# One LayerNorm's three reductions moved one output block later, and an input mean made without VectorE's help

## What is computed

```
h = layer_norm(x, ln_in_g, ln_in_b)
for each of 2 layers:
    z = h @ w_in                                  # 2048 columns, split into 8 parts
    A: a_val * sigmoid(a_gate) -> depthwise conv, width 31 -> layer_norm -> silu
    B: u = gelu(b_u); v = layer_norm(gelu(b_v), ln_v_g, ln_v_b); u * (tril(w_s) @ v + b_s)
    C: c_b * conv3(c_c * c_x)
    D: (trailing window means - token) @ w_pool * pool_scale
    h = layer_norm(ALPHA * h + concat(A, B, C, D) @ w_out)
    h = layer_norm(ALPHA * h + ffn(h))            # layer 0 dense SwiGLU, layer 1 eight experts, top 2
```

## Time and profile before

| | |
|---|---|
| time, median of 3 runs | 1467.56 us (1467.43 to 1468.27) |
| time of the profiled execution | 1467.36 us |
| its span, first to last instruction | 1465.6 us |
| TensorE matmul busy | 1451.2 us, 99% |
| weight loads into TensorE busy | 1259.8 us, 86% |
| VectorE busy | 1226.8 us, 84% |
| ScalarE busy | 962.8 us, 66% |
| GpSimd busy | 117.5 us, 8% |
| memory traffic | 300 GB/s over the span |
| mean granted TensorE clock | 0.999 of full speed |

### The profile page before, as it was taken

One profiled execution on the slowest core, in us unless ns is written; L12 is line 12 of the kernel. 1 busy time (PEld: TensorE's weight loads), 2 busy tenths in 40 slices (PEclk: granted clock), 3 DMA queues, 4 the chain that ended last, 5 costly groups with the idle time before them and its releaser, 6 DMA issues.

```text
span 1465.6 us, 20270 instructions
## 1 busy us (share of the span) xinstructions
PE 1451.2 (99%) x7821; PEld 1259.8 (86%) x7821; DVE 1226.8 (84%) x1206; ACT 962.8 (66%) x912; POOL 117.5 (8%) x131
## 2 busy tenths in 40 slices
PE   9999999999999999999999999999999999999998
PEld 8979999999997888888888888888888888788887
DVE  7987555555698899998999888898889899999886
ACT  5755333334475677777777777777777777777774
POOL 3522000000024000001000001000000101200000
PEclk9999999999999999999999999999999999999999
DMA  9736544454343699999999999999999999999991
GB/s 352 166 119 205 174 151 167 151 174 168 108 136 132 231 376 393 364 390 394 387 367 385 371 384 367 419 363 380 374 367 392 398 376 398 401 368 364 375 375 64
DMA packets 68601, 440.48 MB, mean 301 GB/s; under 512 B 9568, under 2 KB 13600, under 8 KB 17184
## 3 DMA queue, kind: packets, MB, share of 16 engines
q1 hardware_dynamic: 60464, 424.69, 76.7%
q0 software_dynamic: 5120, 13.37, 3.0%
q10 hardware_dynamic: 2928, 1.18, 0.4%
HBM read 432.12 MB, written 7.09 MB: 300 GB/s over the span
## 4 chain that ended last, share of the span: by engine, by line
PE 91%; DVE 5%; ACT 2%; issue 1%; DMA 0%; POOL 0%; DVEq 0%; SPq 0%; ACTq 0%; POOLq 0%
PE bank L951 60%; PE bank L607 22%; PE bank L755 4%; PE bank L989 2%; DVE w_lo L1427 1%; DVE w_lo L2077 1%; DVE work L1633 1%; ACT w_hi L1116 0%; PE bank L941 0%; PE bank L932 0%; DMA h<-in_x_t 0%; ACT h_tok_hi L1286 0%; DVE r_tok L2041 0%; ACT w_hi L1352 0%; PE bank L542 0%
## 5 line engine op out<-in xcount | busy, mean ns | idle before, releaser
L2077 DVE TENSOR_TENSOR w_lo<-ring,w_hi 128x2048 fp32r<-128x2048 f32 x320 | 731.2, 2290 | 79.7 <-ACT w_hi L1352 76.5
L1352 ACT ACTIVATE w_hi<-ring 128x2048 fp32r<-128x2048 f32 x320 | 613.5, 1918 | 163.4 <-PE bank L951 163.2
L951 PE MATMUL bank<-w_hi,x_hi 128*128 128x512 f32 x896 | 354.1, 395 | 1.5 <-DVE w_lo L2077 1.3
L951 PE MATMUL bank<-w_hi,x_lo 128*128 128x512 f32 x896 | 349.3, 390 | 0.0
L951 PE MATMUL bank<-w_lo,x_hi 128*128 128x512 f32 x896 | 348.5, 389 | 0.0
L951 PEld LDWEIGHTS bank<-w_hi,x_hi 128*128 128x128 f32 x896 | 168.3, 188 | 36.6 <-issue 1.9
L951 PEld LDWEIGHTS bank<-w_hi,x_lo 128*128 128x128 f32 x896 | 168.2, 188 | 35.8
L607 PE MATMUL bank<-x_hi,w_hi 128*128 128x290 f32 x656 | 196.4, 299 | 0.5 <-DVE w_lo L1427 0.5
L951 PEld LDWEIGHTS bank<-w_lo,x_hi 128*128 128x128 f32 x896 | 168.4, 188 | 33.2
L607 PE MATMUL bank<-x_lo,w_hi 128*128 128x290 f32 x656 | 195.1, 297 | 0.0
L607 PE MATMUL bank<-x_hi,w_lo 128*128 128x290 f32 x656 | 194.7, 297 | 0.0
(11 more groups left out here) (327 smaller groups left out, 1731.9 us busy)
## 6 DMA issues: line engine op xcount, KB each, us to landing
ring<-in_w_e_gate SPq DMA_DIRECT2D x112, 1024.0 KB, 7.2
ring<-in_w_e_up SPq DMA_DIRECT2D x112, 1024.0 KB, 7.3
ring<-in_w_e_down SPq DMA_DIRECT2D x112, 1024.0 KB, 7.3
ring<-in_w_in SPq DMA_DIRECT2D x15, 1024.0 KB, 5.0
ring<-in_w_ff_gate SPq DMA_DIRECT2D x14, 1024.0 KB, 4.9
ring<-in_w_ff_up SPq DMA_DIRECT2D x14, 1024.0 KB, 4.9
ring<-in_w_ff_down SPq DMA_DIRECT2D x14, 1024.0 KB, 4.9
ring<-in_w_out SPq DMA_DIRECT2D x8, 1024.0 KB, 7.7
```

Source lines behind the costliest of these rows:

```text
L951: ins = mm(out, x, w[slot][:, columns], start=(first and n == 0), stop=(last and n == 2), skip_group_check=True)
L1352: A(w_hi[(CUT0 + p) % SPLIT][:, :], ring[(START + p) % SLOTS][:, :], ACT.Copy).then_inc(hi_done, 1)
L2077: V.tensor_tensor(w_lo[(CUT0 + p) % SPLIT][:, :], ring[(START + p) % SLOTS][:, :], w_hi[(CUT0 + p) % SPLIT][:, :].bitcast(F32), ALU.subtra ...
```

## The change

The input mean takes all eight blocks by TensorE alone; VectorE's three additions and the semaphore between them are gone. In both layers the three reductions of the v norm stand behind blocks 8, 10 and 12, where they stood behind 7, 9 and 11. VectorE's list in the mixer is as it was.

```
-                for b in left if summed else range(KB // 2) if name == "in" else range(nb):
+                for b in left if summed else range(nb):
                     ready(b)
                     last = mm(bank[MEAN_BANK[name]][:, 0:TOKENS], ones[:, :], x[:, b, :],
                               start=(b == 0 and not summed), stop=(b == left[-1] if summed else b == nb - 1))
-                if name == "in":
-                    pe.wait_ge(x_summed, KB // 2 - 1)
-                    last = mm(bank[MEAN_BANK[name]][:, 0:TOKENS], ones[:, :], sq[:, 0, :], start=False, stop=True)
...
-                for n in range(4, 8):
+                for n in range(4, 14):
                     z_block(layer, n, c0)
-                next(ln_v)
-                for n in range(8, 10):
-                    z_block(layer, n, c0)
-                next(ln_v)
-                for n in range(10, 12):
-                    z_block(layer, n, c0)
-                next(ln_v)
-                for n in range(12, 14):
-                    z_block(layer, n, c0)
+                    if n in (8, 10, 12):
+                        next(ln_v)
...
-            dve.wait_ge(x_in[1], 16)
-            for b in range(KB // 2 + 1, KB):
-                if b > KB // 2 + 1:
-                    dve.wait_ge(x_summed, b - KB // 2 - 1)
-                V.tensor_tensor(sq_l[:, 0, :], h[:, KB // 2, :] if b == KB // 2 + 1 else sq_l[:, 0, :], h[:, b, :],
-                                ALU.add).then_inc(x_summed, 1)
```

More of the change, by code:

```diff
@@ L332, in build @@
         h_scaled, h_done, sq_summed = sem("h_scaled"), sem("h_done"), sem("sq_summed")
-        x_summed = sem("x_summed")
         ln_spread = sem("ln_spread")
```

## The result

The changed kernel takes 1470.55 us (median of 18 runs, 1469.82 to 1471.77), the kernel before 1467.66 us (18 runs, 1467.33 to 1468.27): ratio 1.0020, 95% interval 1.0014 to 1.0027, 2.9 us slower. The forecast was +1.8.

What follows compares the result with a forecast made beforehand. TensorE was taken to bound the kernel, with VectorE nearly full beside it in the first mixer. Input mean 0.73, layer 0 0.45 and layer 1 0.6 made +1.8 us on 1467.36: 1469.2 us, range 1466.5 to 1470.8.

Steps and rivals of the forecast that it cites:

- its own case: Whole kernel: input mean and both mixers together cost 1.8 us, giving 1469.2 us, range 1468.2 to 1470.2; chance 61%.
- the uncushioned rival: Mixers: TensorE's slack before the a means is missing, VectorE's delay goes through whole, +3.2 us, 1470.6 us; chance 9%.
- the input's share: Launch: four new matmuls replace VectorE's additions, the input mean is ready 0.73 us later and everything behind it moves.
- The contention rival: Mixers: delayed VectorE has one or two more taps per layer slowed by GpSimd, up to 0.52 us each; chance 8%.
- The stalls before the v mean: Both mixers: block 8 fills TensorE's wait for VectorE's pair sum, removing 0.91 us in layer 0 and 0.69 in layer 1.
- block 12: Both mixers: TensorE waits 0.8 us there for VectorE's late cut of the low weight part.
- the spread's move: Mixers: three transposes one block later cost nothing, since pooling covers VectorE between its cut and the scaling.
- The a norm of layer 0: Layer 0: late pair sum starts the a mean 0.35 us later, plus 0.1 after a stall: +0.45 us.
- The rival that counts the removed stalls in full: Mixers: removed stalls of 0.91 and 0.69 us count whole against the input's +0.73, giving 1466.5 us; chance 16%.
- Layer 1, the same way: Layer 1 mixer: variance 1.62 us late, a mean 0.49 later after slack, plus 0.1 for the stall: +0.6 us.
- TensorE's slack of 1.13: Layer 1: time between when VectorE's pair sum would allow the a mean and its start, absorbing part of VectorE's delay.
- the upper bound 1.26: Input mean: price of the four new matmuls if they ran like the first eight records' 2.51 us, instead of 0.73.

Runs made afterwards that it cites:

- the second experiment: The kernel before with only the v norm's reductions moved behind blocks 8, 10 and 12, input mean as before: 1469.93 us, ratio 1.0015.
- the input edit: The changed kernel with the v norm back behind blocks 7, 9 and 11, so only the input mean by TensorE alone: 1469.12 us, ratio 1.0009.
- the thinned changed kernel: The changed kernel with GpSimd's 24 side additions cut to one column each: 1468.25 us, ratio 1.0004.
- the two with one late reduction: Kernel before with only the v mean behind block 8: 1468.96 us; or with only the variance behind block 10: 1471.73 us.
- the cold kernel before: The kernel before without the eight warm-up matmuls TensorE runs before x lands: 1469.41 us, ratio 1.0011.
- the last two: Kernel before, input sum split five blocks TensorE, three VectorE, v mean mid-block 8: in layer 1 only 1466.48 us; in both layers 1467.52 us.
- the kernel with the mean in mid-block: The kernel before with the v mean in the middle of block 8 in both layers, the rest as before: 1466.88 us, ratio 0.9996.

## Why the prediction was nearly right

The forecast was 1469.2 us in a range to 1470.8, no change beyond 0.2%. The measured ratio, 1.0020, stands on that very bound, at +2.9 instead of +1.8, and the median lies within the range. It lies outside the 1468.2 to 1470.2 that the prediction gave its own case, though: the range reached so far only for the uncushioned rival (1470.6), whose sign, an a mean of layer 0 over 0.9 later than the input's share, measured 0.39. The contention rival's 1470.2 to 1471.3 holds the median, and its cause was there. So the forecast's place within the range is in part luck. Step by step:

**Right, with their sizes.** The stalls before the v mean are gone. Centring is late by 0.42 in layer 0 and 0.70 in layer 1 (forecast 0.40 and 0.61), the variance by 1.11 and 1.66 (0.88 and 1.62), TensorE stands 0.95 and 0.7 at block 12 (0.8), the spread's move costs nothing: VectorE's scaling starts at 435.02 without idle time before it. The a norm of layer 0 has moved by 0.49 (0.45). The rival that counts the removed stalls in full is out: with its cause alone the second experiment is slower by 2.3 us.

**Right in size, in part by another cause.** The variance of layer 0 is late, but the row has no wait: six taps took 1.44 longer beside GpSimd's masks. Without that VectorE would have come at 51.4 and waited for the sum, which ended at 52.54 (51.89 + 0.65). The sum by itself makes 0.8 of the 1.11, as forecast, and the slowed taps added only 0.3.

**Mis-sized: layer 1.** The step "Layer 1, the same way" had +0.6 for the a mean and the trace has +1.26. It carried the variance's delay to the a pair sum and took off TensorE's slack of 1.13, with all VectorE work between as long as before. The runs put 1.09 us more there, of VectorE beside GpSimd's additions, and a stand of 0.9 in the output projection, which TensorE doesn't get back. So the a mean of layer 1 was set by TensorE and not, as forecast, by VectorE's pair sum, which was itself 2.09 late instead of 1.62. The contention rival named this cause, by one or two taps of 0.52 in each layer. What was missing is that it is not a matter of one more tap that meets an addition: a whole stretch goes over from GpSimd slowed to VectorE slowed, and it did so in one layer of the changed kernel and not in the other.
The Trainium skill, in "SBUF — State Buffer", section "Who interferes with whom", has "Issue order, not op shape, decides who blocks". The traces agree in so far as the same instructions are slowed now on one side and now on the other, additions at 0.95 us each beside taps at 0.44, or additions at 0.79 beside taps at 0.82; that the order of issue decides it, no run here shows.

**Mis-sized: the input mean.** Forecast +0.73 at 0.247 us a record. The four new matmuls did run at 0.24 a record; the first eight did not keep their 2.51 us. The cost is 0.4 to 0.6 with the clock early at its upper level (the input edit and the thinned changed kernel centre at 9.17 and 8.94) and 1.55 with it late, and +1.5 in the median of the edit alone. The prediction had the upper bound 1.26 from the first records' mean; it read 2.51 us for eight as "a start-up" of the run, where by the spacing it was the clock, and took that part as fixed while it is the part that varies.

**Not foreseen.** The low clock in the routing of layer 1, +0.6 to 0.8 where it occurs. It is in the profiled execution of after and not in that of before, but in launches of both kernels, and no part of the +2.9 is shown to be its.

**Still open.** Which side is slowed in a layer I can say only afterwards. In layer 0 it came in the five kernels whose v mean or variance had moved there and whose input was centred at 8.5 to 9.0 us, and not in the changed one, centred at 10.1; what shift of VectorE against ScalarE's products sets it was not measured by itself. In layer 1 it came in exactly the three kernels whose variance stood a block later. Nor was the routing's clock: it fell in the profiled executions of after, of the two with one late reduction, of the cold kernel before and of the last two, and not in the other eight, and neither the time of the routing nor the edit sorts them; nor does TensorE's busy time just before (2.87 of 4 us from 488 in after, and as much from 484 in the kernel with the mean in mid-block, where the clock did not fall). No experiment separates its cause.

## What to carry to other kernels

When two engines are nearly full, a stall removed from the one by making the other's input later is paid for in the other's list: fill the gap with so little work that the other engine's input stays on time (half a block, 1.6 us, here), not with a whole block; even that paid in one layer only. VectorE beside GpSimd's additions had two prices, and a shift of under a microsecond can move a whole stretch from one to the other; price such a delay by both, and look at the additions' spacing to see which holds. At the start of a launch read the pace of matmuls from their starts, and don't move a sum onto TensorE where its cover by another engine would hide a late clock.

## What the hardware showed beyond expectation

The same sixteen records took 4.15, 5.32 and 6.84 us: the first two behind the same warm-up matmuls, the third without them. The spacing is 0.48 us, then 0.24. Behind the same warm-up the change-over fell at 5.4 us in the kernel before and at 7.2 in the changed one, while the granted clock read 1.00 in both; it read 1.00 without the warm-up too.

GpSimd's additions and VectorE's instructions settle for a whole stretch into one of two patterns, with VectorE's time for the same list 24.3 to 24.8 or 25.7 us. No kernel at full width lay between.

In six of fourteen profiled executions the granted clock read 0.57 to 0.98 in one or two neighbouring stretches of 4 us in the routing (488 to 500 us), with TensorE busy all through it in the changed kernel's row, and the end came 0.6 to 0.8 us later than in the kernel before's. Its mark in the mean over the span, 0.998, stands in 20 of 91 launches of the kernel before.
